# First norms from squares added on VectorE, with a later context, and transitions in two parts

## The reference

```python
def rmsnorm(x, g):
    y = x * lax.rsqrt(jnp.mean(x * x, axis=-1, keepdims=True) + 1e-6)
    return y * g
mod   = jax.nn.silu(c) @ w_mod + b_mod           # (6 * 1024), and mod_c from c_ctx
h  = rmsnorm(x,   norm1_g) * (1 + sc1)  + sh1    # 512 tokens
hc = rmsnorm(ctx, norm1_g) * (1 + sc1c) + sh1c   # 256 context tokens
... = split(h @ w_in), split(hc @ w_in)
# later, in each half of the second block
x = x + rms_norm(f, post_g);  h = rms_norm(x, pre_g);  h @ w
```

## Time and profile before

| what | value |
|---|---|
| median of three runs | 2908.97 us (2908.12 to 2909.49) |
| the profiled execution | 2907.14 us |
| its span | 2905.3 us |
| TensorE busy | 2827.4 us, 97% |
| VectorE busy | 1290.8 us, 44% |
| ScalarE busy | 1131.3 us, 39% |
| POOL busy | 1186.1 us, 41% |
| mean granted TensorE clock | 0.995 |

### The profile page before, as it was taken

One profiled execution on the slowest core, in us unless ns is written; L12 is line 12 of the kernel. 1 busy time (PEld: TensorE's weight loads), 2 busy tenths in 40 slices (PEclk: granted clock), 3 DMA queues, 4 the chain that ended last, 5 costly groups with the idle time before them and its releaser, 6 DMA issues.

```text
span 2905.3 us, 34409 instructions
## 1 busy us (share of the span) xinstructions
PE 2827.4 (97%) x13708; PEld 2242.9 (77%) x13708; DVE 1290.8 (44%) x1714; ACT 1131.3 (39%) x1681; POOL 1186.1 (41%) x539
## 2 busy tenths in 40 slices
PE   7999999999999999999999999999999999999999
PEld 6787678788888776787787888867767868788887
DVE  4776424511113866835315202277677353341123
ACT  4334643432233555433334222245545233432222
POOL 2123233344443662453443444435624434344443
PEclk9999999999999999999999999999999999999999
DMA  7343223333333211232232323332102323233232
GB/s 255 116 152 126 76 83 99 110 113 96 96 100 125 80 59 37 72 94 73 88 123 77 98 94 102 95 104 79 66 30 73 102 66 110 93 98 99 94 95 80
DMA packets 89278, 277.97 MB, mean 96 GB/s; under 512 B 9952, under 2 KB 10272, under 8 KB 89120
## 3 DMA queue, kind: packets, MB, share of 16 engines
q1 hardware_dynamic: 89120, 275.78, 29.4%
HBM read 268.40 MB, written 7.34 MB: 95 GB/s over the span
## 4 chain that ended last, share of the span: by engine, by line
PE 87%; DVE 9%; ACT 3%; issue 1%; SPq 0%; DMA 0%; DVEq 0%; ACTq 0%
PE bank L1640 24%; PE bank L1642 24%; PE bank L1641 24%; PE bank L1750 2%; PE bank L1943 2%; PE bank L1893 2%; PE bank L1665 1%; PE bank L1666 1%; PE bank L1667 1%; PE bank L1905 1%; PE bank L1934 1%; DVE pageR L2640 1%; DVE pageF L2775 1%; PE bank L1710 1%; PE bank L1880 1%
## 5 line engine op out<-in xcount | busy, mean ns | idle before, releaser
L2913 POOL TENSOR_TENSOR wlo<-wraw,whi 128x1024 fp32r<-128x1024 f32 x429 | 1039.9, 2427 | 1489.5 <-ACT whi L1972 1482.1
L1640 PE MATMUL bank<-pageR,whi 128*128 128x512 f32 (+1 forms) x3376 | 1366.7, 405 | 20.0 <-DVE pageR L2640 8.2
L1642 PE MATMUL bank<-pageR,wlo 128*128 128x512 f32 (+1 forms) x3376 | 1306.4, 387 | 0.0
L1641 PE MATMUL bank<-pageR,whi 128*128 128x512 f32 (+1 forms) x3376 | 1305.5, 387 | 0.0
L1640 PEld LDWEIGHTS bank<-pageR,whi 128*128 128x128 f32 x3376 | 636.0, 188 | 186.7 <-issue 60.3
L1641 PEld LDWEIGHTS bank<-pageR,whi 128*128 128x128 f32 x3376 | 636.8, 189 | 143.6 <-issue 24.0
L1642 PEld LDWEIGHTS bank<-pageR,wlo 128*128 128x128 f32 x3376 | 635.4, 188 | 131.6
L1972 ACT ACTIVATE whi<-wraw 128x1024 fp32r<-128x1024 f32 x429 | 450.5, 1053 | 408.7 <-PE bank L1642 343.3
L2056 ACT ACTIVATE pageR<-pageF 128x512 fp32r<-128x512 f32 x136 | 86.0, 632 | 444.8 <-DVE pageF L2634 196.1
L2775 DVE SCALAR_TENSOR_TENSOR pageF<-pageF,prm 128x497 f32<-128x497 f32 (+9 forms) x180 | 200.0, 1111 | 2.7
L2629 DVE TENSOR_TENSOR pageF<-bank,pageF 128x512 f32<-128x512 f32 x44 | 30.4, 690 | 212.9 <-PE bank L1642 209.0
(11 more groups left out here) (239 smaller groups left out, 2305.6 us busy)
## 6 DMA issues: line engine op xcount, KB each, us to landing
wraw<-in_wst SPq DMA_DIRECT2D x429, 512.0 KB, 3.5
pageF<-in_wmod SPq DMA_DIRECT2D x96, 256.0 KB, 4.5
pageF<-in_xT SPq DMA_DIRECT2D x16, 256.0 KB, 4.4
pageF<-in_bias SPq DMA_DIRECT2D x16, 256.0 KB, 3.9
kept<-pageF SPq DMA_DIRECT2D x16, 256.0 KB, 4.5
pageF<-kept SPq DMA_DIRECT2D x16, 256.0 KB, 4.0
out_x<-pageF SPq DMA_DIRECT2D x8, 256.0 KB, 2.0
pageF<-in_cT SPq DMA_DIRECT2D x4, 256.0 KB, 6.4
```

The costliest lines, as they stand in the source:

```text
L1640: e.matmul(o, hi, xh, start=first, stop=False)
L1641: e.matmul(o, hi, xl, start=False, stop=False)
L1642: i = e.matmul(o, lo, xh, start=False, stop=last)
L2913: e.tensor_tensor(wlo[:, b % NH, :, :], wraw[:, b % NR, :, :], bc(whi[:, b % NH, :, :]), ALU.subtract).then_inc(*wlod.up(("wlo", b)))
```

## The change

The context is loaded behind modulation group 1. The x squares are still ScalarE's, but VectorE adds them page to page, and TensorE multiplies only the sum with one column of ones; root and spread are made as in the later norms. The context's squares, root and spread stand inside `first_products`, its inputs behind them, and its products for k below 4 are held back until the end of step 3. Warming products stand behind the first columns and before the first inputs. The order of `h_in` and `h_lo` is by pairs. In `wide`, every step now has the two products with the input's first part for all four items, then those with its remainder; splits are planned only in steps 0 and 5 to 7; `root` stands between the two parts of step 7, `spread` behind it.

```diff
@@ wide
-            for (name, m), o in zip(items, outs):
-                s = self.w_next((name, m, k))
-                self.step("mm", s, ((o, xs[k]),), k == 0, k == 7)
-                if late is not None and k == 6 and o is outs[-1]:
-                    late[0]()
-                if late is not None and k == 7 and o is outs[-1]:
-                    late[1]()
+            slots = [self.w_slot((name, m, k)) for name, m in items]
+            if k == 0 or k > 4:
+                self.w_ahead(*slots)
+            self.step("mm_first_part", tuple(slots), tuple(outs), xs[k], k == 0)
+            if late is not None and k == 7:
+                late[0]()
+            self.step("mm_second_part", tuple(slots), tuple(outs), xs[k], k == 7)
+            if late is not None and k == 7:
+                late[1]()
+            for _ in items:
                 yield
...
@@ planned
-    for k in range(4):
-        pages.take(("XC", k))
-        step("load_ctx", k)
     step("load_fixed", "prm")
     for q in range(4):
         if q < 3:
             p.w_load(q)
         for k in range(8):
             mod_load(8 * q + k)
+        if q == 1:
+            for k in range(4):
+                pages.take(("XC", k))
+                step("load_ctx", k)
...
+    def first_squares(t, n):
+        for k in range(n):
+            pages.take(("q", t, k))
+            step("first_square", t, k)
+            if k:
+                step("square_add", t, k, 512)
+                pages.give(("q", t, k), ("qa", t, k))
+
+    def first_rows(t, n, width):
+        sbk.take(("qm", t))
+        p.row_of[t] = len(p.row_of)
+        step("first_rows", t, n)
+        pages.give(("q", t, 0), ("qm", t))
+        step("root", t, 1024, False, width)
+
+    def first_spread(t, width):
+        step("spread", t, width)
+        pages.take(("r", t))
+        step("spread_page", t, width)
+        sbk.give(("qm", t), ("rr", t))
...
+    first_squares("x", 8)
+    step("log_exp")
+    first_rows("x", 8, 4)
+    p.keep_warm(sbk, 2)
     p.w_split(0)
+    first_spread("x", 4)
     step("load_fixed", "wal")
     step("load_fixed", "tabG")
+    mod_rows(0)
+    mod_columns(0)
+    p.keep_warm(sbk, 3)
+    inputs(0)
     step("first_norms")
-    mod_rows(0)
-    step("rstd_dve", "x", T, 1024)
...
     p.w_split(1)
@@ first_products
-        rows, turned = {(0, 2): 1, (1, 3): 2, (3, 1): 3}, {(1, 0): 1, (2, 1): 2, (3, 3): 3}
+        rows, turned = {(0, 3): 1, (2, 3): 2, (4, 0): 3}, {(1, 1): 1, (3, 1): 2, (4, 2): 3}
+        late = []
         for k in range(8):
             for i, (name, m, ctx) in enumerate(items):
+                if (k, i) == (2, 3):
+                    first_rows("ctx", 4, 2)
+                if (k, i) == (3, 0):
+                    first_spread("ctx", 2)
+                    for q in range(2):
+                        inputs_ctx(q)
+                if (k, i) == (3, 3):
+                    inputs_ctx(2)
...
+                    if q == 1:
+                        first_squares("ctx", 4)
+                    elif q == 3:
+                        inputs_ctx(3)
...
+                if ctx and k < 4:
+                    late.append((s, ("oc", name, m), k))
+                elif ctx:
+                    groups.append((("oc", name, m), HC[k]))
...
+            if k == 3:
+                for name, m, ctx in items[1:]:
+                    sbk.take(("oc", name, m))
+                for s, o, kk in late:
+                    step("mm", s, ((o, HC[kk]),), kk == 0, False)
+                    if kk % 2:
+                        yield
@@ TensorE
+            def mm_first_part(slots, outs, x, first):
+                xh = half(x, "hi")
+                w.wait_ge(*when(*x, "hi"))
...
+                    e.matmul(bank(name), whi[:, b % NH, j, :], xh, start=first, stop=False)
+                    e.matmul(bank(name), wlo[:, b % NH, j, :], xh, start=False, stop=False)
+
+            def mm_second_part(slots, outs, x, last):
+                xl = half(x, "lo")
+                w.wait_ge(*when(*x, "lo"))
...
+                    i = e.matmul(bank(name), whi[:, b % NH, j, :], xl, start=False, stop=last)
...
-            def first_sums():
...
+            def first_rows(t, n):
+                o, x = bank(("qm", t)), F(("q", t, 0))
+                clear(("qm", t))
                 w.wait_ge(*when("cst"))
+                w.wait_ge(*when("qa", t, n - 1))
+                width = 4 if t == "x" else 2
+                for j in range(4):
+                    i = e.matmul(o[:, j % width:j % width + 1], x[:, 128 * j:128 * j + 128], ones[:, 0:1], start=j == 0,
+                                 stop=j == 3, skip_group_check=True)
+                i.then_inc(*dot.up(("qm", t)))
```

More of the change, by code:

```diff
@@ L340, in rows @@
                 p.pages.give(("q", t, i), ("qm", t))
-        p.step("root", t, n, self.tail is not None)
+        p.step("root", t, n, self.tail is not None, 4)
     def rstd_rows(self, n, bks):
@@ L348, in rstd_rows @@
         p.keep_warm(bks, 1)
-        p.step("spread", t)
+        p.step("spread", t, 4)
         p.keep_warm(bks, 3)
@@ L455, in hc_lo, with inputs, inputs_ctx @@
         pages.give(("hct", k), ("HC", k, "hi"), ("HC", k, "lo"))
[L457 to L468, removed]
+    def inputs(q):
+        for k in (2 * q, 2 * q + 1):
+            h_in(k)
+        for k in (2 * q, 2 * q + 1):
+            h_lo(k)
+    def inputs_ctx(q):
+        for k in (2 * q, 2 * q + 1):
+            hc_in(k)
+        for k in (2 * q, 2 * q + 1):
+            hc_lo(k)
+    first_squares("x", 8)
+    step("log_exp")
+    first_rows("x", 8, 4)
+    p.keep_warm(sbk, 2)
     p.w_split(0)
+    first_spread("x", 4)
     step("load_fixed", "wal")
     step("load_fixed", "tabG")
+    mod_rows(0)
+    mod_columns(0)
+    p.keep_warm(sbk, 3)
+    inputs(0)
     step("first_norms")
-    mod_rows(0)
-    step("rstd_dve", "x", T, 1024)
[L475 to L483, removed]
     p.w_split(1)
@@ L980, in spread @@
             t = ("in", self.gain)
-            step("spread", t)
+            step("spread", t, 4)
             pages.take(("r", t))
-            step("spread_page", t)
+            step("spread_page", t, 4)
             sbk.give(("qm", t), ("rr", t))
@@ L1626, in clear, with mm @@
                     w.wait_ge(*when(*k))
-            def mm(s, groups, first, last):
+            def mm(s, groups, first, last, final=True):
                 b, j = divmod(s, 8)
@@ L1727, in square_rows, with spread @@
                 x.then_inc(*dot.up(("qm", t)))
-            def spread(t):
+            def spread(t, width):
                 o, r = bank(("qm", t)), rows(t, 0)
                 w.wait_ge(*when("rcol", t))
-                for j in range(4):
+                for j in range(width):
                     x = e.matmul(o[:, 128 * j:128 * j + 128], r[:, j:j + 1].broadcast_to([128, 128]), ident, start=True,
@@ L1992, in rstd_act, with root @@
                 e.activation(r, r, ACT.Exp, scale=-0.5).then_inc(*fun.up(("re", t)))
-            def root(t, n, two):
-                x, r = rows(t, 2), rows(t, 0)
+            def root(t, n, two, width):
+                x, r = rows(t, 2)[:, 0:width], rows(t, 0)[:, 0:width]
                 log_exp()
+                w.wait_ge(*when("prm"))
                 w.wait_ge(*when("qs", t))
@@ L2280, in scalar @@
             mine = {f.__name__: f for f in (
-                silu_c, w_split, square, log_exp, rstd_act, root, spread_page, ret_turned, x_square, first_norms, mod_row, h_in, hc_in, halves, evict,
+                silu_c, w_split, square, log_exp, rstd_act, root, spread_page, ret_turned, first_square, mod_row, h_in, hc_in, halves, evict,
                 evict_half, evict_turned, evict_z,
@@ L2323, in rstd_dve, with root @@
                 e.scalar_tensor_tensor(r, x, 1.5, r, ALU.add, ALU.mult).then_inc(*vec.up(("rr", t)))
-            def root(t, n, two):
+            def root(t, n, two, width):
                 o = bank(("qm", t))
-                r, s, x = (rows(t, i) for i in range(3))
+                r, s, x = (rows(t, i)[:, 0:width] for i in range(3))
                 w.wait_ge(*when("qm", t))
@@ L2889, in vector @@
             mine = {f.__name__: f for f in (
[L2890 removed]
+                first_norms, square_add, rstd_dve, root, mod_columns, h_in, h_lo, hc_in, hc_lo, halves, rope_gla,
                 gla_gate, gla_gate_ctx, gla_scan, gla_decays, gla_state0, gla_states, gla_scores, gla_normed, na_normed, na_bias, soft_exp, soft_sums, na_out, mla_out, silu_gate, mod_acc,
```

88 lines of the change are left out of this document (29 added, 59 removed).

## The result

The changed kernel took 2917.33 us (median of 7 runs, 2916.40 to 2920.59), the kernel before, timed beside it, 2909.05 us (7 runs, 2908.12 to 2911.02). The ratio is 1.0027, 95% interval 1.0018 to 1.0036. That is 3.8 us above the forecast of 2913.5 and just beyond the upper end of its range, 2917.0: the direction beyond 0.2% that I had given 22%.

What follows compares the result with a forecast made beforehand. TensorE, busy 97% of the span, was taken as the bound. Start -2.6, fed transitions +6.6 and the unfed stretch +0.5 summed to +4.5 us: 2913.5 us against the median of 2908.97, range 2894 to 2917.

Steps and rivals of the forecast that it cites:

- The fed transitions: Three wide stretches: three queued POOL splits hold the root's small operations, TensorE idles 4.4 us; +2.2 us each, +6.6 in all.
- the rival in which they slip between: At the root in fed transitions: small VectorE operations get through between POOL splits; -13.1 us, 2895.9, chance 0.24.
- The clock, forecast 1.95 us a transition: Behind the 4.4 us hole in each fed transition: TensorE's granted clock falls, costing 1.4 to 2.9 us, taken as 1.95.
- the forecast of +0.25 a transition: Each fed transition without clock loss: the late spread and new hole against the removed waits, +0.25 us, +0.8 in all.
- The start: Up to 60 us: earlier first product and saved clock against context work, new holes and a collision; -2.6 us in sum.
- my lower bound of -4.6: At the start: the most it could gain, -4.6 us, if VectorE and ScalarE keep ahead.
- 0.9 and 1.1: At the start: two new TensorE holes, 0.9 us before input 2 and 1.1 us at the context's columns.
- The stretch without feed: Wide stretch at 925 us: columns move behind step 7's first parts, so the spread comes at 929.1 instead of 928.62; +0.5 us.
- The clock stays whole: Fed transitions: the hole is there but the clock stays at 2.4 GHz; -1.3 us, 2907.7, chance 0.11.
- the change of order does nothing: Fed transitions: VectorE's pace of 2.65 us a step sets them, so no effect there; -2.1 us, 2906.9, chance 0.06.
- the worst case: The start gives nothing, with a second low clock, and transitions lose 2.9 us of clock each; +10 us, 2919, chance 0.09.

Runs made afterwards that it cites:

- the starved run: The changed kernel with splits planned in steps 0 and 5 only, so one split instead of three stands ahead of the root: 2932.48 us.

## Why the prediction was right or wrong

**The fed transitions, forecast +6.6, measured +9.3 in the profiles.** The mechanism was right in each of its steps, and each has a run behind it: three splits back to back (7.01 us; I had 7.1), L2336 and L2338 both held (1.56 and 2.26 us as L2382 and L2384), a hole of 3.86, 3.50 and 3.86 us (I had 4.4), and a clock of 0.5 behind it. That the splits make the hole is shown by taking them away (0.36); that POOL's end, not the root's place, sets the spread is shown by moving the root; that one split fewer in the last queue brings back the time of the kernel before is shown by planning one in every step. The gain that the change was built on is real too: remainder 5 at 0.74, and the third hole, for ScalarE's half, gone.

The Trainium skill, page "SBUF — State Buffer", section "Who interferes with whom", has such a pair of instructions exclude each other whole. The trace agrees: L2382 and L2384 each end within 0.1 us of the end of a POOL split, down to operations of four elements, and the rival in which they slip between was wrong.

**The clock, forecast 1.95 us a transition.** Here lies the step that failed: I let the clock fall behind the three holes and nowhere else. The run with warming products in the holes gives the sizes. Behind the first and the third hole the clock cost 2.34 and 2.42 us. In the second stage one can follow the same products in both profiles. The changed kernel is 2.64 us behind that run at the columns of 1900.62, 3.87 at the spread behind the hole (1937.34), 4.79 at 1948.07 and 6.39 at 2247.67. So the clock behind the second hole cost 0.9 us, and the three together 5.7, where I had 5.9. The rest lies where I had put nothing:

```profile
1903.00:1909.00 6.00, 6.00 (x17) 3.70 (x17) 2.39 (x8) 0.56 (x3) 0.00 (x0) 0.50 0.18 59
2244.00:2248.00 4.00, 4.00 (x12) 3.13 (x11) 2.08 (x3) 2.59 (x3) 0.95 (x1) 0.57 0.41 131
```

The first of these low stretches stands ahead of the second hole, behind small columns and a pause of 0.71 us, and cost 1.2 us. The second follows a pause of 2.13 us long after the transition, and cost 1.6. The same two stretches of the kernel before have both pauses (0.72 and 2.13 us) and a granted clock of 1.00. A third, ahead of the last fed transition (0.57 over 2534 to 2538), is in the run with warming products too. From columns to first product these two profiles take 8.18 and 8.20 us there, against 7.09 ahead of the first fed transition, and that is the likely source of the +0.85. The profile of the changed kernel's `wide` alone has low stretches in the same three places, the kernel before and the new start alone have none. Why the clock falls there after the change, no run shows. With the clock taken out, the forecast of +0.25 a transition stands against -0.05, -0.02 and +0.85.

**The start, forecast -2.6, measured -0.25 at 67 us.** The step that failed is "I put the page of roots at 18.8. Modulation group 0 is the later one: 18.7 + 1.6 = 20.3 for the first scaling". It came at 22.69. The columns started at 13.12 and the root was done at 16.38, early enough; but the warming products ran until 18.37, the spread until 19.5, and only then, in the same queue, came the 64 products of group 0, all of them, where before only the last eight were left when their tiles landed. I let two things run side by side that stand one behind the other on TensorE. That I had the tiles landed by 18.7 was right: the eighth landed at 18.5. But removing the warming showed that the wait in the queue is not the whole of it. The 64 products then began at 18.48 and took 3.25 us instead of 1.95, so my lower bound of -4.6 was out of reach for a reason that I had not weighed. The rest came as forecast: holes of 0.87 and 0.75 where I had 0.9 and 1.1, and the first product at full clock; over 30 to 60 us TensorE was busy for 27.81 us against 27.97.

**The stretch without feed, forecast +0.5.** Columns at 930.00 and spread at 932.35 are 2.35 us apart, with a hole of 0.36:

```profile
930.00 0.95 PE L1781 MATMUL bank<-cst,pageF 128*128 128x1 f32 x8
...
932.35 1.16 PE L1789 MATMUL bank<-cst,smal 128*128 128x128 f32 x8 [0.36 <-DVE smal L2386]
```

From the columns of the root before it (542.72) to the mark behind it the changed kernel needs 0.69 us more (399.44 against 398.75), and with the root ahead of step 7 only 0.08 more. Right.

**The sum.** -2.6 + 6.6 + 0.5 = +4.5 was forecast. The profiles give -0.25 + 9.3 + 0.7 = 9.75, and 3.4 more in the rest of the first block, which is not the change's (below). The medians give 8.3. "The clock stays whole" and "the change of order does nothing" fell with the slip. Of the worst case one half was true, that the start gives nothing, and that with the low clock away from the holes is what took the time past my range.

## What to carry to other kernels

Work that is left out of one place is only moved: find where it queues next, and which small operation on the way to the bounding engine meets it there, for a chain of operations of four elements can be held longer than the large ones that it frees. A hole in TensorE of 3.5 to 3.9 us cost its length and 0.9 to 2.4 us more in lost clock, so price both, and leave room for a low clock in stretches away from the hole. Where the hole can't be closed, filling it with products that nobody needs gave back 2.3 to 3.8 us a stage, but the same products cost 2.85 us where there was no hole.

## What the runs showed of the hardware that I had not expected

The fall of the clock is not a function of the hole's length alone. Behind holes of 2.95, 2.98 and 2.98 us of one execution it stayed at 2.4 GHz once and fell twice; behind 1.9 us it fell once in three; behind 3.46 to 3.86 it fell in all nine cases, three each in the changed kernel, with its `wide` alone and without the first warming.

The place of a low stretch differs as well, and that moves other work. The hole of 4.88 us at 79 us is in both kernels. Over 80 to 84, 84 to 88 and 88 to 92 us the granted clock is 0.93, 0.50 and 0.72 in the kernel before, and 0.52, 0.63 and 1.00 in the changed one: it falls sooner and comes back sooner. With that TensorE is ahead, and POOL's next split starts 1.6 us earlier (96.23 against 97.81), under a group of VectorE products with two SBUF inputs, and these take longer. VectorE's timeline, before and changed:

```profile
92.31 5.27 DVE L2575 SCALAR_TENSOR_TENSOR pageF<-pageF,csil 128x512 f32<-128x512 f32 x4
```

```profile
92.07 7.20 DVE L2611 SCALAR_TENSOR_TENSOR pageF<-pageF,csil 128x512 f32<-128x512 f32 x4
```

TensorE then waits 1.75 us at 107.6: an earlier clock ends in a later product. The long form stands also in the kernel with the old start (7.37 us) and the short one in the kernel with the new start alone (5.25), so it is no effect of the change. Nor is the next step: between 254 and 261 us the changed kernel falls 3.0 us behind the run with warming products, which has the same start, and the granted clock is 0.51 there against 1.00. At the columns near 540 us (542.72 in the changed kernel) the eight profiles with the new start and its first warming lie between 538.6 and 542.8, the starved run left out, so no single profile should be used to judge the start.

At the very start the small products and the warming products run at half pace (3.76 us for four, against 2.74 for six at 22.02) although the granted clock in the profile shows no fall there. Without the warming the 64 modulation products are stretched instead (3.25 us against 1.95), again at a granted clock of 1.00.
